# Key, query and gate products of a float32 kernel: one 512-column product over high and low features, with the halves added on VectorE

## The reference, cut to what matters

```python
proj = h @ w_in                      # pool mixer: u, gate = proj[..., :2048], proj[..., 2048:]
... (mixed * jax.nn.silu(gate)) @ w_out
kv = h @ w_kv                        # keys and values: 3 groups x 16 heads x 64
proj = h @ w_in                      # dilated mixer: queries of 3 groups, and a gate
scores = jnp.einsum('bnqrhd,bnkrhd->bnrhqk', qb, kb) * (HEAD_DIM ** -0.5)
```

## Time and profile before

| | |
|---|---|
| median of 3 runs | 1578.31 us (1578.15 to 1578.55) |
| the profiled execution | 1574.28 us, of which the span is 1572.3 us |
| TensorE matmul busy in the span | 1524.1 us (97%), 9482 matmuls |
| VectorE | 865.8 us (55%) |
| ScalarE | 675.7 us (43%) |
| GpSimd | 173.6 us (11%) |
| HBM read | 231.22 MB, 148 GB/s over the span |

### The profile page before, as it was taken

The page is one execution under the profiler, slowest core; times in us unless marked ns, Lnnn a source line. Parts: engine busy times, 40 slices in busy tenths (PEclk is TensorE's granted clock), DMA queues, the critical chain, the costliest instruction groups (busy, mean ns, idle before and its releaser), DMA issues.

```text
span 1572.3 us, 24065 instructions
## 1 busy us (share of the span) xinstructions
PE 1524.1 (97%) x9482; PEld 1290.7 (82%) x9482; DVE 865.8 (55%) x1484; ACT 675.7 (43%) x1089; POOL 173.6 (11%) x181
## 2 busy tenths in 40 slices
PE   9999899999999989999899999999999999999998
PEld 7998698999997765786789777777787877779887
DVE  6785664555455865437565433424348646665544
ACT  5454345444444434425554222322224546644443
POOL 2200220000000110001414001110011120011010
PEclk9999999999999989999999999999999999999999
DMA  6456554454436315311213443535422421155451
GB/s 252 182 189 231 214 216 173 175 188 140 183 131 245 113 61 212 128 54 54 81 62 127 161 170 151 207 128 201 171 97 91 138 81 54 68 174 214 172 202 56
DMA packets 43769, 233.80 MB, mean 149 GB/s; under 512 B 13264, under 2 KB 14224, under 8 KB 16784
## 3 DMA queue, kind: packets, MB, share of 16 engines
q1 hardware_dynamic: 31232, 222.38, 37.9%
q10 hardware_dynamic: 12432, 9.94, 2.2%
HBM read 231.22 MB, written 1.08 MB: 148 GB/s over the span
## 4 chain that ended last, share of the span: by engine, by line
PE 82%; DVE 10%; ACT 3%; POOL 2%; issue 2%; DMA 1%; SPq 0%; DVEq 0%; ACTq 0%
PE ps L553 23%; PE ps L555 22%; PE ps L554 22%; PE ps L770 5%; DVE wlo L1079 3%; PE ps L656 3%; PE ps L742 2%; PE ps L708 2%; PE ps L700 2%; ACT whi L1069 1%; DVE nmax L1882 1%; POOL flo L2410 1%; PE ps L618 1%; PE ps L640 1%; DMA raw<-in_wstream 1%
## 5 line engine op out<-in xcount | busy, mean ns | idle before, releaser
L1079 DVE TENSOR_TENSOR wlo<-raw,whi 128x2048 fp32r<-128x2048 f32 x162 | 383.9, 2393 | 245.3 <-ACT whi L1069 245.0
L1069 ACT ACTIVATE whi<-raw 128x2048 fp32r<-128x2048 f32 x162 | 305.1, 1906 | 215.8 <-PE ps L555 163.8
L553 PE MATMUL ps<-fhi,whi 128*128 128x256 f32 (+1 forms) x1216 | 371.6, 306 | 5.5 <-DVE wlo L1079 3.9
L555 PE MATMUL ps<-fhi,wlo 128*128 128x256 f32 (+1 forms) x1216 | 367.9, 303 | 0.0
L554 PE MATMUL ps<-flo,whi 128*128 128x256 f32 (+1 forms) x1216 | 367.8, 302 | 0.0
L553 PEld LDWEIGHTS ps<-fhi,whi 128*128 128x128 f32 x1216 | 232.1, 191 | 29.0 <-issue 9.5
L554 PEld LDWEIGHTS ps<-flo,whi 128*128 128x128 f32 x1216 | 232.3, 191 | 8.8
L555 PEld LDWEIGHTS ps<-fhi,wlo 128*128 128x128 f32 x1216 | 232.2, 191 | 8.9
L553 PE MATMUL ps<-whi,fhi 128*128 128x512 f32 (+1 forms) x624 | 221.7, 355 | 9.4 <-DVE wlo L1079 2.8
L555 PE MATMUL ps<-whi,flo 128*128 128x512 f32 (+1 forms) x624 | 217.3, 348 | 0.0
L554 PE MATMUL ps<-wlo,fhi 128*128 128x512 f32 (+1 forms) x624 | 217.3, 348 | 0.0
(11 more groups left out here) (259 smaller groups left out, 1812.4 us busy)
## 6 DMA issues: line engine op xcount, KB each, us to landing
raw<-in_wstream SPq DMA_DIRECT2D x210, 1024.0 KB, 5.0
gates<-gated ACTq DMA_DIRECT2D x6, 512.0 KB, 4.5
hx<-in_x SPq DMA_DIRECT2D x1, 1024.0 KB, 5.3
lnrow<-in_ln_g ACTq DMA_DIRECT2D x2, 512.0 KB, 4.0
lnrow<-in_ln_b ACTq DMA_DIRECT2D x2, 512.0 KB, 5.4
hc<-in_ctx ACTq DMA_DIRECT2D x1, 1024.0 KB, 5.4
mix<-in_rpb_rows ACTq DMA_DIRECT2D x4, 256.0 KB, 4.3
hc<-in_rpb_rows ACTq DMA_DIRECT2D x4, 256.0 KB, 4.0
```

Of the source, the lines that this page charges most:

```text
L553: mm(o, lh, rh, start=start, stop=False)
L555: return mm(o, ll, rh, start=False, stop=stop)
L1069: nc.scalar.activation(whi[:, w % SPLIT_SLOTS, :], raw[:, c % RAW_SLOTS, :], ACT.Copy).then_inc(*did("scalar", ("hi", w)))
L1079: nc.vector.tensor_tensor(wlo[:, w % SPLIT_SLOTS, :], raw[:, c % RAW_SLOTS, :], whi[:, w % SPLIT_SLOTS, :].bitcast(F32), ALU.subtract).the ...
```

## The change

`by_halves` takes the place of `by_feature` for the gates, and for the keys and queries of the dilated attention. `fhi` and `flo` become the halves of one tile. One matmul of 512 columns (256 of high, 256 of low features) passes over the high weights and fills the whole bank; one of 256 columns over the low weights adds to its first half. VectorE then adds the two halves with a reduction from PSUM (`sum_parts`). For the gates ScalarE's Silu follows on the sum in SBUF; for keys and queries ScalarE's copy is gone, and the queries' factor 1/8 goes into the split of their weights. The 16 gate tiles, 12 tiles ahead of the attention and 36 beside it are of this kind, 64 in all. The values stay as they were.

```diff
+        parts_f = tile(ctx, "f", [P, 2, KD, 512], F32R)
+        fhi, flo = parts_f[:, 0, :, :], parts_f[:, 1, :, :]
...
+            def by_halves(u, name, c0, feat=None, tiles=range(4), side=0):
+                for e in tiles:
+                    o = job(*name, e, side=side)
+                    both = o.rearrange("p (a b) -> p a b", a=2)
+                    for k in range(KD):
+                        if e == 0:
+                            wait_weights(u, k)
+                        if feat and e == 0:
+                            wait_feature(feat, k)
+                        wh, wl = whalf(whi, u, k, e * P, e * P + P), whalf(wlo, u, k, e * P, e * P + P)
+                        if k == KD - 1:
+                            mm(o[:, 0:S], wl, fhi[:, k, c0:c0 + S], start=False, stop=False)
+                        ins = mm(both, wh, parts_f[:, :, k, c0:c0 + S], start=k == 0, stop=k == KD - 1)
+                        if k < KD - 1:
+                            mm(o[:, 0:S], wl, fhi[:, k, c0:c0 + S], start=False, stop=False)
...
-                nc.scalar.activation(whi[...], raw[...], ACT.Copy)
+                nc.scalar.activation(whi[...], raw[...], ACT.Copy, scale=QSCALE if SPLIT[w][0].name[0] == "q" else 1.0)
...
+                if SPLIT[w][0].name[0] == "q":
+                    ins = nc.vector.scalar_tensor_tensor(out=low, in0=raw[...], scalar=QSCALE, in1=high,
+                                                         op0=ALU.mult, op1=ALU.subtract)
...
     (ScalarE, gates)
-                    act.wait_ge(*after("gate", g, e))
-                    copy(sgate[:, g * 4 + e, :], src("gate", g, e)[:, 0:S], ACT.Silu)
+                    act.wait_ge(*after("gate sum", g * 4 + e))
+                    copy(sgate[:, g * 4 + e, :], sgate[:, g * 4 + e, :], ACT.Silu)
     (VectorE, gates)
             split_to(("gate", 0))
             pooled(0)
+            def sum_parts(dst, *label):
+                return v.reduce_sum(dst, src(*label).rearrange("p (a b) -> p b a", a=2), AX_X)
             for g in range(4):
                 split_to(("gate", g))
                 if g == 1:
                     pooled_lo(0)
+                for e in range(4):
+                    dve.wait_ge(*after("gate", g, e))
+                    sum_parts(sgate[:, g * 4 + e, :], "gate", g, e)
             pooled(1)
             pooled_lo(1)
     (VectorE, attend, in iteration i)
                     for at, step in steps:
                         if at == i and first_of_unit(step):
                             split_to(first_of_unit(step))
...
                     for at, step in steps:
+                        if at == i and step[0] in ("k", "q"):
+                            projected(*step)
     (VectorE, ahead of the attention)
                 for g in range(NG):
                     split_to((what, 0, g))
+                    for n in range(2 if what != "v" else 0):
+                        projected(what, 0, g, n)
```

More of the change, by code:

```diff
@@ L584, in by_token @@
                     ins.then_inc(*did("tensor", *labels))
+            def by_halves(u, name, c0, feat=None, tiles=range(4), side=0):
[13 more added lines that the diff above has]
+                            mm(o[:, 0:S], wl, fhi[:, k, c0:c0 + S], start=False, stop=False)
+                    labels = [name + (e,)] + ([("used", u.n)] if (e + 1) * P == u.width else [])
+                    ins.then_inc(*did("tensor", *labels))
             def by_feature(u, name, c0, c1, feat=None, tiles=range(4), side=0, first=True, last=True):
@@ L808, in attend @@
                         elif at == i:
-                            by_feature(UNIT[step[:3]], step[:3], 0, S, tiles=[step[3]], side=1)
+                            by_halves(UNIT[step[:3]], step[:3], 0, tiles=[step[3]], side=1)
                     for m in mods_at(i, items, mods):
@@ L824, in _ @@
             for g in range(4):
-                by_feature(UNIT[("gate", g)], ("gate", g), 0, S, feat=None if g else "fx")
+                by_halves(UNIT[("gate", g)], ("gate", g), 0, feat=None if g else "fx")
             def group(g):
@@ L870, in _ @@
                 for g in range(NG):
-                    by_feature(UNIT[what, 0, g], (what, 0, g), 0, S, feat="f1" if (what, g) == ("k", 0) else None,
-                               tiles=range(2))
+                    by_halves(UNIT[what, 0, g], (what, 0, g), 0, feat="f1" if (what, g) == ("k", 0) else None, tiles=range(2))
             for g in range(NG):
@@ L1068, in split_hi @@
                     act.wait_ge(*after("used", SPLIT[w - SPLIT_SLOTS][0].n))
-                nc.scalar.activation(whi[:, w % SPLIT_SLOTS, :], raw[:, c % RAW_SLOTS, :], ACT.Copy).then_inc(
+                nc.scalar.activation(whi[:, w % SPLIT_SLOTS, :], raw[:, c % RAW_SLOTS, :], ACT.Copy,
+                                     scale=QSCALE if SPLIT[w][0].name[0] == "q" else 1.0).then_inc(
                     *did("scalar", ("hi", w)))
@@ L1078, in split_lo @@
                 nc.vector.wait_ge(*after("hi", w))
-                nc.vector.tensor_tensor(wlo[:, w % SPLIT_SLOTS, :], raw[:, c % RAW_SLOTS, :],
-                                        whi[:, w % SPLIT_SLOTS, :].bitcast(F32), ALU.subtract).then_inc(
-                    *counts.used(c, ("lo", w)))
+                low, high = wlo[:, w % SPLIT_SLOTS, :], whi[:, w % SPLIT_SLOTS, :].bitcast(F32)
+                if SPLIT[w][0].name[0] == "q":
+                    ins = nc.vector.scalar_tensor_tensor(out=low, in0=raw[:, c % RAW_SLOTS, :], scalar=QSCALE, in1=high,
+                                                         op0=ALU.mult, op1=ALU.subtract)
+                else:
+                    ins = nc.vector.tensor_tensor(low, raw[:, c % RAW_SLOTS, :], high, ALU.subtract)
+                ins.then_inc(*counts.used(c, ("lo", w)))
                 state[0] += 1
@@ L1159, in _ @@
                 for e in range(4):
-                    act.wait_ge(*after("gate", g, e))
-                    copy(sgate[:, g * 4 + e, :], src("gate", g, e)[:, 0:S], ACT.Silu).then_inc(
-                        *did("scalar", ("sgate", g * 4 + e), ("read", "gate", g, e)))
+                    act.wait_ge(*after("gate sum", g * 4 + e))
+                    copy(sgate[:, g * 4 + e, :], sgate[:, g * 4 + e, :], ACT.Silu).then_inc(
+                        *did("scalar", ("sgate", g * 4 + e)))
             def u_hi(g):
@@ L1275, in projected @@
                     return
+                if what in ("k", "q"):
+                    return
                 act.wait_ge(*after(what, qr, g, n))
-                dst = {"k": kq1[:, qr % 2, 0, g * 2 + n, :], "q": kq1[:, qr % 2, 1, g * 2 + n, :], "v": v1[:, qr % 2, n, g, :]}[what]
-                copy(dst, src(what, qr, g, n)[:, 0:QW], ACT.Copy, scale=QSCALE if what == "q" else 1.0).then_inc(
-                    *did("scalar", (what + "1", qr, g, n), ("read", what, qr, g, n)))
+                copy(v1[:, qr % 2, n, g, :], src(what, qr, g, n)[:, 0:QW], ACT.Copy).then_inc(
+                    *did("scalar", ("v1", qr, g, n), ("read", what, qr, g, n)))
             def load_bias(n):
@@ L1774, in _ @@
                     pooled_lo(0)
+                for e in range(4):
+                    dve.wait_ge(*after("gate", g, e))
+                    sum_parts(sgate[:, g * 4 + e, :], "gate", g, e).then_inc(
+                        *did("vector", ("gate sum", g * 4 + e), ("read", "gate", g, e)))
             pooled(1)
@@ L1872, in _, with projected @@
             mod_row(*MODS["k", 0, 0][1])
+            def projected(what, qr, g, n):
+                dve.wait_ge(*after(what, qr, g, n))
+                sum_parts(kq1[:, qr % 2, "kq".index(what), g * 2 + n, :], what, qr, g, n).then_inc(
+                    *did("vector", (what + "1", qr, g, n), ("read", what, qr, g, n)))
             def maxima(i, it):
```

2 lines of the change are left out of this document (removed).

## The result

The changed kernel takes 1614.86 us (median of 4 runs, 1612.76 to 1615.42), against 1578.43 us (4 runs, 1578.15 to 1579.02) for the kernel before on the same chip: ratio 1.0236, with a 95% interval of 1.0222 to 1.0249, or 36.4 us more. The forecast was 1613.0 (+34.9).

The account below looks back on a forecast made before the run. TensorE, busy 97% of the span, was taken as the bound. Gates +6.7, tiles ahead -1.2, beside the attention +24.6 and clock +4.8 gave +34.9 us on 1578.3: 1613 us, range 1594 to 1628.

Parts of the forecast that it names:

- TensorE's gain: All 64 tiles: new pair 0.347 us against 0.360 for three small matmuls, 0.10 us per tile, 6.5 us if TensorE-bound.
- that rival: Rival for all 64 tiles: a merged product costs as one of 256 columns; at most -61 us, 1517; chance 0.01.
- The added sums: VectorE's 64 reductions from PSUM: 0.62 us in a row, 0.65 plus about 0.1 hand-over alone; queries' low split 2.29 us.
- Slow sums: Rival: sums take 1.3 us each, gates +11 and about +8 in the attention's waits: 1632 us; chance 0.07.
- Gates: Gates: a loop of sums, Silus and splits moves ScalarE's pooled features from 61.13 to 67.7; +6.7 us at 93 us.
- Ahead of the attention: 12 key and query tiles made before the attention, sums hidden by splits three units ahead: -1.2 us.
- Beside the attention: Dilated attention: sums stand behind low splits with two banks, TensorE waits; +9.2, +7.8 to 8, +7.5 by round, together +24.6 us.
- The lags at v00: Attention: VectorE's lag makes product v00 wait for a query tile's sum, 2.1 us in round one, 1.8 in the next.
- The clock: Attention: TensorE's clock drops to 1.2 GHz behind three long waits (6.9, 5.1, 5.1 us): +4.8 us, bounds 0 and some 10.
- The rival in which only the start binds: Rival: only the gate chain and iteration 0's wait come, other waits are caught up: +8.9, 1587 us; chance 0.12.
- the one in which TensorE's gain shows: Rival: the sums are hidden in VectorE's idle time and TensorE's 6.5 us gain shows: 1572 us; chance 0.04.
- the theory: Attention: sums cost time because they stand behind splits with two banks; side sums made twice would add 8 us (6 to 12).

Follow-up runs that it names:

- the run without sums: Changed kernel without any sums, ScalarE reading each bank's first half, the half of high weights times low features left out: 1572.95 us, ratio 0.9973 to the kernel before.
- the last run: Kernel with sums before splits and gates' order mended, plus the two halves of each feature tile laid next to each other: 1575.93 us, ratio 0.9991.
- when alone: Changed kernel with the 36 key and query products beside the attention as before, gates and 12 tiles ahead as changed: 1582.65 us, ratio 1.0037.
- the doubled sums: Changed kernel with each of the 36 sums beside the attention made twice: 1632.36 us, ratio 1.0345.
- the one with the gates' order mended: Changed kernel, gates reordered: unit 0's sums before first pooled features, next high splits before Silus from unit 1, second pooled features before last sums: 1607.88 us.
- the kernel with both orders mended: Changed kernel with side sums ahead of the low splits beside the attention and the gates' order mended, all sums kept: 1577.08 us, ratio 0.9996.

## Why the prediction was right, and where its sizes were off

**TensorE's gain: the step was mis-sized.** Forecast 0.347 us per pair, 0.10 per tile. The first pairs of the gates, on TensorE's timeline:

```profile
19.05 0.40 PE L601 MATMUL ps<-f,whi 128*128 128x512 f32 x1
...
19.40 0.40 PE L601 MATMUL ps<-f,whi 128*128 128x512 f32 x1
...
19.75 0.40 PE L601 MATMUL ps<-f,whi 128*128 128x512 f32 x1
```

0.35 from start to start, and 0.352 as a mean of 50 to 60 pairs later: 0.065 per tile, 4.1 us for the 64 and not 6.5. Adding up the paces of two uniform streams was 5 ns per pair too good; that is small, but the gain itself was only 13 ns. What the 5 ns are isn't settled: the run without sums shows that it isn't the readers of the banks, the last run that it isn't the layout. The Trainium skill (TensorE: Matmul & The Clock Gate, Back-to-back issue gap) gives N/2.4 + 2.5 ns for an isolated matmul; an estimate by it has the pair at 325 ns and the three small ones at 328. The trace's 352 and 360 disagree: both paces are longer, and the gain between them is larger. No run shows a merged product at the price of a small one; that rival is gone.

**The added sums: right.** 0.682 us each by the profile, and 0.62 in a row (four in 2.48). "Slow sums" fell. The queries' low split takes 2.29 us (rows at 360.20), as said; the mean of 2.64 in the group holds those that run beside GpSimd. The sums from 44.04 on run while GpSimd has an addition of 3.63 us from 44.20, and take 2.48 like the others: no contention, where two low splits stretched to 8.09. The Trainium skill (SBUF — State Buffer, Who interferes with whom) says this of tensor_reduce, and the trace agrees.

**Gates: right.** 67.7 was forecast for the pooled features, 67.31 came; +6.7 at the wait, +6.16 came. By the medians the gates cost 6.3 (undone), and 6.7 when alone (5.9, with the gain of the 12 tiles added). Between the two profiles 1.5 us of low clock behind that wait come on top, which the step didn't have. But this clock isn't tied to the sums: it follows the wait of 2.34 us in the run without any sums as well.

**Ahead of the attention:** -1.2 forecast, about -0.3 by the positions at its start; -0.8 by the measured pace. The positions hold another difference: behind the wait at 190.95 the granted clock is 0.50 up to 196, some 5 us, and before it is back at 187, some 4 us behind the wait at 183.30.

**Beside the attention: right in mechanism, sizes off both ways.** The waits at the third products of iterations 0, 8 and 16 came at 6.60, 4.99 and 4.99 (6.9, 5.1, 5.1 forecast; 5.0 without iteration 0's longer queue). The waits for a release with one product between were 2.20, 2.18 and 2.20 where 2.3, 2.3 and 3.3 were said. The lags at v00 gave 1.20 and 1.21, for 2.1 and 1.8. So the waits were over-estimated by 3.6 us in all (30.1 forecast, 26.5 measured; its first round adds up to 9.3, not 9.2). In the other direction, 1.3 us less gain on the side tiles and a fourth stretch of low clock. The stretch is 31.55 us longer, and the sum of its rows, 26.5 of idle less the old 1.2, plus 6.8 of clock, less 2.3 of gain, is 29.8. The 1.7 that are missing are 0.17 per wait. That is about what the brackets leave out: they count from the end of the matmul before, whose row shows 0.39 or 0.40 us, while matmuls of its kind start 0.23 apart.

**The clock: right for the three waits that were named, and one drop short.** 4.8 us forecast; the products behind the three took 1.75, 2.0 and 1.5 us longer than at the full 2.4 GHz, 5.2 in all. The product behind the 2.20 us wait at 305.28 took 4.44 us in place of 2.82, another 1.6. The forecast had left the shorter waits to its upper bound.

**The order of the argument** held as far as it was tested: the same sums in another place cost 5 us instead of 36, a third bank takes away most as well, and undoing either half of the change gives its forecast share. The rival in which only the start binds fell (three rounds of waits, not one), and so did the one in which TensorE's gain shows: even without any sums it is 3.8 us. That the total was met within 2 us is partly luck: too long lags (3.6 us) on one side, too much gain, a fourth drop of the clock and the clock at 100 us on the other. And the theory alone failed for the doubled sums, where it put waits right but nothing for the clock behind them.

## What to carry to other kernels

An engine that is busy 55% of the time can still be the one that is waited for: before work is given to it, look at what stands ahead of that work in its program, what that in turn waits for, and how many banks the producer has until it must wait. Count the clock behind a wait with the wait: here four drops cost 6.8 us on top of 26.5 of waiting. Put the read that frees a bank ahead of work that itself waits for the producer. And price the gain first, over the instructions that lie on the path only: here 13 ns per pair were hoped for, 8 came, a quarter of the tiles lay off the path, and even with both orders mended short waits and the clock behind one of them left nothing that could be told.

## What the runs showed of the hardware that had not been expected

- The granted clock after a short wait isn't the same each time. In the changed kernel, and in the one with the gates' order mended, the wait of 2.47 us is followed by the 1.2 GHz level; in the kernel with both orders mended the same wait, at the same place, is not. At this place the run without sums waits 2.34 us and has the low clock behind it; the kernel before and the one with the gates undone wait 2.35 us and don't. Windows of the kernel with the gates' order mended, and of the one with both:

```profile
94.00:96.00 2.00, 2.00 (x12) 2.00 (x11) 2.00 (x3) 0.04 (x1) 0.00 (x0) 0.50 0.74 209
```

```profile
94.00:96.00 2.00, 2.00 (x19) 2.00 (x18) 2.00 (x3) 0.05 (x1) 0.00 (x0) 1.00 0.65 197
```

  12 matmuls against 19 in the same 2 us, for some 1.5 us of loss. The wait of 1.58 us with the sums ahead of the splits is followed by it in each of the three kernels that have it, and every wait of 3.8 us or more in the attention is. What decides it for the shorter ones these runs don't show.
- A pair of one 512-column and one 256-column product, each with its weights, takes 0.352 us, not the 0.347 that the two kinds give by themselves (0.227 and 0.120), whatever the distance between the halves.
- A reduction over two halves of a bank taken crosswise runs at the pace of one over 512 elements in order: 682 ns against 684.
